# Attention in a hybrid diffusion layer: q, k, v and the probabilities in upper and lower parts, with three products each

## The reference

```
q = rms_norm(q.reshape(b, L, H_Q, HD), p['q_norm'])
k = rms_norm(k.reshape(b, L, H_KV, HD), p['k_norm'])
...
qr, kr = apply_rope(q, cos, sin), apply_rope(k, cos, sin)
...
    k_all = jnp.concatenate([ctx_k.astype(kr.dtype), kr], axis=1)
    v_all = jnp.concatenate([ctx_v.astype(v.dtype), v], axis=1)
...
s = jnp.einsum('bqgrd,btgd->bgrqt', qi, k, preferred_element_type=jnp.float32) * scale
p = jax.nn.softmax(s, axis=-1).astype(v.dtype)
return jnp.einsum('bgrqt,btgd->bqgrd', p, v)
```

## Time and profile before

| | us |
|---|---|
| median of 3 runs | 1854.9 |
| lowest and highest run | 1849.82, 1855.33 |
| the profiled execution, by the same clock as the runs | 1860.62 |
| its span in the trace | 1858.9 |

### The profile page before, as it was taken

The page is one execution under the profiler, slowest core; times in us unless marked ns, Lnnn a source line. Parts: engine busy times, 40 slices in busy tenths (PEclk is TensorE's granted clock), DMA queues, the critical chain, the costliest instruction groups (busy, mean ns, idle before and its releaser), DMA issues.

```text
span 1858.9 us, 27421 instructions
## 1 busy us (share of the span) xinstructions
PE 1638.2 (88%) x11141; PEld 1542.0 (83%) x11141; DVE 1031.8 (56%) x1419; ACT 662.4 (36%) x1099; POOL 99.5 (5%) x155
## 2 busy tenths in 40 slices
PE   4799999989998997888789899989289999999995
PEld 2699989889998987787755599989289999999995
DVE  5466675557754676786465353434934353342467
ACT  3544443334373265655455442321131121111210
POOL 1000012110101100000000000000000000000000
PEclk9799998999998999988899999999689999999998
DMA  9344355442486666664520164333102222223221
GB/s 306 98 128 139 126 172 195 131 136 65 153 268 235 211 208 222 179 205 163 181 106 23 46 199 148 115 139 112 45 24 69 70 74 71 79 68 90 68 68 56
DMA packets 159721, 241.14 MB, mean 130 GB/s; under 512 B 8048, under 2 KB 126560, under 8 KB 156576
## 3 DMA queue, kind: packets, MB, share of 16 engines
q1 hardware_dynamic: 136464, 171.45, 28.5%
q0 software_dynamic: 12304, 47.72, 6.9%
q10 hardware_dynamic: 10880, 20.97, 4.1%
HBM read 195.06 MB, written 45.06 MB: 129 GB/s over the span
## 4 chain that ended last, share of the span: by engine, by line
PE 72%; DVE 15%; ACT 7%; issue 3%; DMA 2%; SPq 0%; ACTq 0%; DVEq 0%
PE acc L805 64%; PE tp L805 5%; DVE arena L1850 2%; DVE wlo L1750 2%; ACT arena L1511 1%; ACT whi L1286 1%; PE tp L1190 1%; DVE arena L2003 1%; DMA arena<-in_w_mod 1%; PE tp L888 1%; DVE arena L1789 1%; DVE arena L1788 1%; ACT arena L1298 1%; DVE wlo L1801 1%; DVE arena L2005 1%
## 5 line engine op out<-in xcount | busy, mean ns | idle before, releaser
L805 PE MATMUL acc<-hh,whi 128*128 128x322 f32 x1408 | 343.3, 326 | 33.3 <-ACT arena L1298 20.1
L805 PE MATMUL acc<-hl,whi 128*128 128x322 f32 x1408 | 336.5, 321 | 0.0
L805 PE MATMUL acc<-hh,wlo 128*128 128x322 f32 x1408 | 333.2, 319 | 0.0
L805 PEld LDWEIGHTS acc<-hh,whi 128*128 128x128 f32 x1408 | 248.0, 199 | 37.1 <-ACT arena L1298 21.7
L805 PEld LDWEIGHTS acc<-hl,whi 128*128 128x128 f32 x1408 | 250.5, 198 | 0.0
L805 PEld LDWEIGHTS acc<-hh,wlo 128*128 128x128 f32 x1408 | 248.8, 197 | 0.0
L1286 ACT ACTIVATE whi<-raw 128x2048 fp32r<-128x2048 f32 x78 | 148.7, 1908 | 266.3 <-PE acc L805 266.3
L1750 DVE TENSOR_TENSOR wlo<-raw,whi 128x2048 fp32r<-128x2048 f32 x78 | 178.5, 2290 | 105.5 <-ACT whi L1286 105.2
L805 PE MATMUL acc<-whi,hh 128*128 128x256 f32 x720 | 207.6, 288 | 7.9 <-DVE hl L2238 7.9
L805 PE MATMUL acc<-whi,hl 128*128 128x256 f32 x720 | 204.3, 284 | 0.0
L805 PE MATMUL acc<-wlo,hh 128*128 128x256 f32 x720 | 204.1, 283 | 0.0
(11 more groups left out here) (255 smaller groups left out, 2331.3 us busy)
## 6 DMA issues: line engine op xcount, KB each, us to landing
raw<-in_w_in SPq DMA_DIRECT2D x38, 1024.0 KB, 7.0
raw<-in_w_mlp SPq DMA_DIRECT2D x32, 1024.0 KB, 5.4
arena<-in_w_mod SPq DMA_DIRECT2D x24, 1024.0 KB, 6.4
arena<-decay_sums_t ACTq DMA_DIRECT2D x40, 512.0 KB, 5.5
arena<-xs_nat SPq DMA_DIRECT2D x8, 1024.0 KB, 8.1
raw<-in_w_ssd_o SPq DMA_DIRECT2D x8, 1024.0 KB, 6.3
y_nat<-arena POOLq DMA_DIRECT2D x6, 1024.0 KB, 7.3
arena<-y_nat SPq DMA_DIRECT2D x6, 1024.0 KB, 5.9
```

Of the source, the lines that this page charges most:

```text
L805: return pe.matmul(out, l, r, start=first, stop=last)
```

## The change

- Each head of q and k is stored as two fp32r parts. ACT's copy becomes the upper part, and DVE subtracts it from what is in PSUM for the lower part (`heads_lower`). POOL stores both. The cached k is treated in the same way.
- v and the cached v are loaded during the last chunk of the scan. ACT copies the upper parts, and DVE subtracts.
- q is no longer loaded whole: it comes one head at a time, in two buffers. k comes in two parts.
- Scores and values are three products of fp32r parts (`thrice`). The values are computed for two steps at a time, 256 columns wide.
- The transposed probabilities are split too: ACT copies them out of PSUM (upper part), DVE subtracts (`probs_lower`).
- ACT does the multiplication by the reciprocal of the sum, in place. DVE computes only the reciprocal (`inverse_sums`).
- The probabilities have three buffers in place of two.
- Some semaphores of the small dt computation are merged.

The core of the diff, PE first:

```diff
+            def thrice(out, l, r, first=True, last=True):
+
+                mul(out, l[0], r[0], first, False)
+                mul(out, l[0], r[1], False, False)
+                return mul(out, l[1], r[0], False, last)
...
-                    q = qT[:, h, t * P:(t + 1) * P]
-                    mul(acc[:, 2 * u, 0:LAT], q, qT[:, HQ + h // R, 0:LAT])
-                    last = mul(acc[:, 2 * u + 1, 0:PAST], q, kcT[:, h // R])
+                    q = [qb[:, h % 2, i, t * P:(t + 1) * P] for i in range(2)]
+                    thrice(acc[:, 2 * u, 0:LAT], q, [k[:, h // R, 0:LAT] for k in (kh, kl)])
+                    last = thrice(acc[:, 2 * u + 1, 0:PAST], q, [k[:, h // R] for k in (kch, kcl)])
...
-                if n % 4 == 1 and 4 < n < N_SCORE:
-                    values(n // 4 - 1)
-            values(HQ - 1)
-            values(HQ)
-            values(HQ + 1)
+                if n % 2 == 0 and n:
+                    values(n // 2 - 1)
+            for j in range(N_SCORE // 2, N_SCORE // 2 + HKV):
+                values(j)
```

ACT, before attention and in its loop:

```diff
+            act.wait_ge(s["av_in"], 32)
+            act.activation(vh[:], vn, ACT.Copy).then_inc(s["v_hi"], 1)
+            act.activation(vch[:], vc, ACT.Copy).then_inc(s["v_hi"], 1)
             weights(F_END)
...
-                if n >= 2:
-                    act.wait_ge(s["p_turned"], n - 1)
+                if n >= 3:
+                    act.wait_ge(s["p_turned"], n - 2)
...
+            def probabilities(n):
+                w = n % 3
+                act.wait_ge(ex["sem"], n + 1)
+                act.wait_ge(sums["sem"], due(sums))
+                if n < N_SCORE:
+                    last = act.activation(pr[:, w], pr[:, w], ACT.Copy, scale=sm[:, w, 12:13])
...
                 if n + 1 < N_SCORE + HKV:
                     exps(n + 1)
-                if n == N_SCORE + 1:
-                    att_out(HQ - 1)
-                probs_out(n)
-                if n % 4 == 1 and 4 < n < N_SCORE:
-                    att_out(n // 4 - 1)
+                if n:
+                    probs_out(n - 1)
+                probabilities(n)
+                if n % 2 == 1 and n > 2:
+                    att_out((n - 3) // 2)
```

DVE, in the q/k/v stage, before attention and in its loop:

```diff
+            def heads_lower(n):
+
+                for h in range(2):
+                    dve.wait_ge(qhi["sem"], due(qhi))
+                    dve.tensor_tensor(qts[:, h, 1, LAT:], tp[:, 2 * h + 1, 0:P], qts[:, h, 0, LAT:].bitcast(F32), ALU.subtract)
+                    dve.tensor_tensor(qts[:, h, 1, 0:LAT], tp[:, 2 * h], qts[:, h, 0, 0:LAT].bitcast(F32),
+                                      ALU.subtract).then_inc(qlo["sem"], step(qlo))
+
             for n in range(2, 5):
                 squared(n)
+                heads_lower(n - 2)
                 rotated(n)
             step(free, NT)
             split_lo(1)
+            heads_lower(3)
...
+            dve.wait_ge(s["v_hi"], 1)
+            dve.tensor_tensor(vl[:], vn, vh[:].bitcast(F32), ALU.subtract).then_inc(s["v_ok"], 1)
+            dve.wait_ge(s["v_hi"], 2)
+            dve.tensor_tensor(vcl[:], vc, vch[:].bitcast(F32), ALU.subtract).then_inc(s["v_ok"], 1)
...
+            def probs_lower(n):
+                dve.wait_ge(phi["sem"], due(phi))
...
+                dve.tensor_tensor(lo_, src, hi_.bitcast(F32), ALU.subtract).then_inc(plo["sem"], step(plo))
...
             maxima(0)
             maxima(1)
+            inverse_sums(0)
             for n in range(N_SCORE + HKV):
-                probabilities(n)
+                if n + 1 < N_SCORE + HKV:
+                    inverse_sums(n + 1)
+                if n:
+                    probs_lower(n - 1)
                 if n + 2 < N_SCORE + HKV:
                     maxima(n + 2)
-                if n % 4 == 1 and 4 < n < N_SCORE:
-                    att_lower(n // 4 - 1)
+                if n % 2 == 1 and n > 2:
+                    att_lower((n - 3) // 2)
```

SP, in the last chunk of the scan:

```diff
+                        for n, k in enumerate((kh, kl)):
+                            sp.dma_start(k[:].bitcast(F32), qkt_d[n, HQ:].rearrange("h p t -> p h t")).then_inc(s["att_in"], 16)
+                        sp.dma_start(kch[:].bitcast(F32).rearrange("p h t -> p (h t)"), kct_d[0]).then_inc(s["att_in"], 16)
+                        sp.dma_start(vn, v_d.rearrange("t p c -> p t c")).then_inc(s["av_in"], 16)
+                        sp.dma_start(vc, hk(a["cache_v"])).then_inc(s["av_in"], 16)
```

More of the change, by code:

```diff
@@ L18 @@
 NT = (CTX + LAT) // P
+NKC = PAST // P
 HQ, HKV, HD = 8, 2, 128
@@ L585, in y_in @@
                 sp.dma_start(yst[:, n % 2], y_d[Y_ORDER[n]]).then_inc(s[f"yt_in{n % 2}"], 16)
-            gate_in(0)
-            gate_in(1)
+            for n in range(2):
+                sp.dma_start(qc[n][:].bitcast(F32), qkt_d[n, 0:HQ].rearrange("h p t -> p h t")[:, :, LAT:]).then_inc(s["qc_in"], 16)
+            for h in range(2, HQ):
+                q_in(h)
+                if h < 4:
+                    gate_in(h - 2)
             sp.wait_ge(s["score_ready"], N_SCORE + HKV)
@@ L711, in heads_out @@
                     po.wait_ge(copied["sem"], due(copied))
-                    po.dma_start(qkt_d[h], qts[:, h % 2]).then_inc(qo[h % 2]["sem"], step(qo[h % 2]))
+                    for n in range(2):
+                        po.dma_start(qkt_d[n, h], qts[:, h % 2, n].bitcast(F32)).then_inc(qo[h % 2]["sem"], step(qo[h % 2]))
             po.wait_ge(s["acst_ok"], 1)
@@ L731, in _ @@
             po.wait_ge(s["qk_copied"], HQ + 1)
-            po.dma_start(kct_d, kct).then_inc(s["kct_out"], 16)
+            for n in range(2):
+                po.dma_start(kct_d[n], kct[n][:].bitcast(F32)).then_inc(s["kct_out"], 16)
             step(copied)
@@ L1161, in _ @@
             pt_turned, pt_free = count(s["p_turned"]), count(s["p_copied"])
-            pe.wait_ge(s["att_in"], 16 * 3)
+            pe.wait_ge(s["att_in"], 16 * 4)
+            qin = [count(s[f"q_in{b}"], 32) for b in range(2)]
+            def thrice(out, l, r, first=True, last=True):
+                mul(out, l[0], r[0], first, False)
+                mul(out, l[0], r[1], False, False)
+                return mul(out, l[1], r[0], False, last)
             def scores(n):
@@ L1189, in turn_p, with values @@
                 for j in range(6 if n < N_SCORE else R):
-                    last = pe.transpose(tp[:, j // 4, (j % 4) * P:(j % 4 + 1) * P], pr[:, u, j * P:(j + 1) * P], ident)
+                    last = pe.transpose(tp[:, j // 4, (j % 4) * P:(j % 4 + 1) * P], pr[:, n % 3, j * P:(j + 1) * P], ident)
                 last.then_inc(pt_turned["sem"], step(pt_turned))
-            def values(h):
+            def values(j):
                 step(pvf)
@@ L1408, in _ @@
             act.wait_ge(s["dt_in"], 48)
[L1409 removed]
+            act.activation(wdh[:], wdt, ACT.Copy).then_inc(s["dt_act"], 1)
             act.activation(alg, alg, ACT.Exp).then_inc(steps["sem"], step(steps))
[L1411 to L1414 removed]
+            act.wait_ge(s["dt_pe"], 1)
+            act.activation(dtt.rearrange("p (a b) -> p a b", a=2), tp[0:2 * NH, 0:2, 0:HALF], ACT.Copy).then_inc(s["dt_act"], 1)
+            qt, qhi, qo = count(s["qk_turned"]), count(s["qk_hi"]), pair("qts_out")
             def block_tile(n, t, dst):
@@ L1465, in _ @@
             act.wait_ge(qt["sem"], due(qt))
-            act.activation(kct, tp[:, 2], ACT.Copy).then_inc(qc["sem"], step(qc))
+            act.activation(kct[0][:], tp[:, 2], ACT.Copy).then_inc(qhi["sem"], step(qhi))
             for c in nat_out + conv_out:
@@ L1600, in exps @@
                     last.then_inc(ex["sem"], step(ex))
+            def probabilities(n):
[4 more added lines that the diff above has]
+                    last = act.activation(pr[:, w], pr[:, w], ACT.Copy, scale=sm[:, w, 12:13])
+                else:
+                    for r in range(R):
+                        p = pr[:, w, r * P:(r + 1) * P]
+                        last = act.activation(p, p, ACT.Copy, scale=sm[:, w, 12 + r:13 + r])
+                last.then_inc(prob["sem"], step(prob))
@@ L1637, in _ @@
                     squares(0, q, z0[:, q * 512:(q + 1) * 512])
-            att_out(HQ)
-            att_out(HQ + 1)
+            probs_out(N_SCORE + HKV - 1)
+            for j in range(N_SCORE // 2, N_SCORE // 2 + HKV):
+                att_out(j)
             roots(ysc[:, 0])
@@ L2051, in gated @@
                 dve.tensor_tensor(y, y, z, ALU.mult).then_inc(sqi["sem"], step(sqi))
+            weights(2)
+            heads_lower(4)
             scaled(0, 0, 0)
-            weights(F_CTX)
+            weights(F_CTX - 2)
             masked()
@@ L2061, in _ @@
                         scaled(0, 0, (g + 1) // 2)
+                    if g == 3:
+                        for o in pair("qts_out"):
+                            step(o, HQ + HKV)
+                            dve.wait_ge(o["sem"], value(o))
                     if g > 1:
```

272 lines of the change are left out of this document (152 added, 120 removed).

## The result

The kernel after takes 1898.1 us (median of 4 runs, 1896.8 to 1899.5), against 1855.1 us of before in the same comparison: a ratio of 1.0232, with a 95% interval of 1.0201 to 1.0262. It is 43 us slower. I had forecast 1879 us, with a range that ended at 1896. The sign and the ring of waits came as forecast, the size didn't.

What follows compares the result with a forecast made beforehand. PE was taken to bound the kernel (72% of the chain) and attention, with short waits. Terms +4.2 + 0.5 + 0.7 + 2.0 + 12.8 + 4 = +24 us gave 1879 us, range 1864 to 1896 us.

Steps and rivals of the forecast that it cites:

- The sum: Whole kernel: all terms together add +24 us, giving 1879 us on the median of 1854.9 us.
- The ring: Attention: ACT's exponential and upper part, DVE's lower part and maximum in series; steps of 3.76 and 4.37 us, +12.8 us.
- two bounds: Attention loop: +3.7 us if PE's 0.6 us never shows, +31 us if each of six links is 0.1 us dearer.
- The clock: Attention loop: PE's pauses lower its clock two or three times, 1.7 us each; +4 us, from 0 to 25.
- The q/k/v stage: `heads_lower(3)` delays PE's gate transposes by 2.6 us and the clock drop costs 1.6 us; +4.2 us, from 0 to 5.
- Ahead of attention: Before the first exponential: upper parts of v less shorter transfer +0.5, moved loads +0.7, lower parts of v +2.0 us.
- The clock's fall in each pair: Rival, attention loop: the clock falls in all 15 pairs of steps, 25 us in place of 4; 1900 us, chance 0.12.
- PE as the pace setter: Rival, attention loop: waits overlap, PE sets the pace and the loop gains 15 us; about 1847 us, chance 0.09.
- PE out of the ring: Rival, attention loop: every step takes 3.76 us and no clock is lost; 1866 us, chance 0.17.
- The signs: Trace after: exponentials 3.7 to 4.4 us apart, maximum right behind lower part, chain mostly ACT and DVE, PE about 70% busy.

Runs made afterwards that it cites:

- the added products: Kernel after plus twelve unused products of 256 columns on PE in each odd attention step from 3 to 29: 1889.5 us, ratio 1.0166.
- the kernel with the maximum first: Kernel after with DVE's maximum of step n + 2 put before the lower part of step n - 1: 1931.6 us, ratio 1.0408.
- The last experiment: Kernel after with the last four subtractions of `heads_lower(3)` done for only an eighth of their columns: 1900.9 us in a single run.

## Why the forecast was too low, step by step

- **The sum.** In the profiled executions +38.5 us stand against +24.2 us forecast. Of the 14.3 us between them the clock is 10.0, the MLP 5.6, the rest of attention 1.7 and the stretch just ahead of it 1.0; what comes before that was 4.0 us better than forecast, less than the 13 us by which executions of the same code differ there.
- **The ring** was right in every link. Forecast 3.76 and 4.37 us, measured 3.77 us (972.33 to 976.10) and 4.26 us (968.07 to 972.33); the lower part of 768 columns took 0.96 us, as estimated. As a term, +12.8 us forecast, +14.5 us measured with the clock held up. In that kernel it is 126.0 us from the first exponential to the first of context (126.5 forecast), and from there to the next stage 16.5 us instead of 14.4 (forecast: as before, within 3). In after these two are 138.5 and 18.1 us. One of its two bounds has a slip: 15 x 7.52 gives +3.6 us, not +3.7.
- **The clock** is the step that failed. It stood in the sum as "I count it twice or three times: +4 us, from 0 to 25", and it cost 14.0 us in attention. The price of one fall was right (1.7 us forecast, 9.6 - 8.04 = 1.56 us measured); the count was wrong: two or three falls forecast, nine pairs of 15 measured. I had a stretch with PE busy for 5.46 us of 8 at full clock, and one with 6.45 us followed by 0.79, and took the milder one for a loop that repeats. The rule cited with the forecast, the Trainium skill's "TensorE: Matmul & The Clock Gate", section "A second HAM failure mode: psum-queue depth-cycling", says that short pauses between groups of matmuls can make the clock oscillate. The trace agrees: in a pair PE pauses once, for 2.3 us, and the granted clock swings between 1.00 and 0.79. That work in the pauses stops the swing is shown by the added products. Which property of the pauses brings it on isn't: the kernel with the maximum first left PE busy for less (5.14 us of 8 from 996 us on) and kept 1.00 there, and the same loop with early parts of v fell in three pairs.
- **The q/k/v stage** was right in place and size: +4.2 us forecast. From the last weights' split to the table load it takes 7.12 us in before, 8.65 us in another execution of the same code, and 11.8 to 12.4 us in all twelve traces that have the change there. PE's transposes for the gates start 2.0 us later than before (507.48 and 509.50 us; 2.6 forecast), and the 48 products behind them take 1.9 us more (1.6 forecast). The last experiment undoes 2.15 us of it. What reaches the next stages can't be read from two traces: the `z_nat` load starts at 900.8 to 914.3 us in twelve traces of the same code there (median 910.0), and at 907.95 and 906.75 us with the code of before.
- **Ahead of attention** +3.5 us against +2.5: the lower parts of v take 2.0 us as forecast (933.70 to 935.71). The upper parts take 1.67 us (916.35 to 918.02), and the shorter transfer gave back only 0.4 us (5.97 against 6.36).
- **The MLP** is the second step that failed: it was not in the sum at all. I had looked at what stands behind each edit on its queue, not at what the added instructions do to a loop far behind them: +6.4 us for three rounds, of which 0.8 came back elsewhere behind attention. Without it the time would have been inside the range, and with the clock as forecast too.
- **The rivals.** The clock's fall in each pair, 1900 us, came nearest, at a chance of 0.12; it was right in kind and too strong in the count (25 us, where 14.0 were measured). That its total fits is in part luck, since it has no term for the MLP. PE as the pace setter and PE out of the ring are refuted by 8.04 and 9.6 us for two steps.
- **The signs.** PE is busy for about 70% of the loop, as forecast (5.66 us of 8 is 71%), and in every other step the maximum starts within 0.1 us of the lower part's end (974.93 and 975.02 us). The exponentials start 3.77 and 4.26 us apart only in the pairs at the full clock; in the other nine the second distance is 5.8 us. The chain didn't go over to ACT and DVE for most of the time: PE holds 53% of it from 936.8 to 1075 us, where it held 75% of before's loop.

## What to carry to other kernels

Before splitting operands into parts to save TensorE time, write down for each engine's queue what stands behind the new instructions, and follow the ring to its end: here a lighter PE load was turned into a ring of 3.77 us a step. When a repeated loop leaves TensorE with a pause in each turn, put the low clock into the sum for many of its turns and not for two or three: here nine pairs of 15 had it. What helped most here was an order that keeps TensorE busy, not fewer products. With the same arithmetic as after, new orders on three queues, values in halves and the parts of v earlier take 1853.4 us, and with 59 idle products that place the MLP's loop 1847.8 us, 0.4% below before (0.2 to 0.6%). Between those two the medians differ by 5.6 us, but single runs of each spread by 11 to 22 us, so this step alone isn't settled. Nor is the MLP all of it: in the profiled runs its three rounds are 2.0 us shorter, and the kernel with 27 idle products, which loads in each round, takes 1850.4 us.

## What the runs showed of the hardware

- Adding products made a kernel faster: 9 us, since the granted clock no longer fell to 0.79 in most pairs but stayed at 1.00.
- The time of a loop depends on where its instructions lie. TensorE's MLP loop loaded 9 instruction packets in each round or none, by the number of instructions ahead of it, and three rounds took 358.6 to 375.7 us; the loads alone don't account for all of this difference.
- Executions of the same code differ by 13 us in the first 910 us. A few microseconds there are read from local distances, not from the span.
